# Two transformer-like blocks on one core: rate rows, wide decay products and a regrouped s5 input

## What is computed

```python
# gated delta rule, chunks of 64 tokens in the reference (the kernel takes 128)
g = jnp.cumsum(chunks(g), axis=-1)                 # g = -exp(a_log) * softplus(alpha_raw + dt_bias)
diff = g[..., :, None] - g[..., None, :]
decay = jnp.where(incl, jnp.exp(jnp.where(incl, diff, 0.0)), 0.0)
L = jnp.where(strict, jnp.einsum('bhnid,bhnjd->bhnij', kb, k) * decay, 0.0)
attn = jnp.einsum('bhnid,bhnjd->bhnij', q, k) * decay
...
# SSD, chunks of 128 tokens
adt = (dt * a)                                     # dt = softplus(dt_raw + dt_bias), per head
a_cs = jnp.cumsum(adt, axis=-1)
seg = a_cs[..., :, None] - a_cs[..., None, :]
lmat = jnp.exp(jnp.where(mask, seg, -jnp.inf))
y_diag = jnp.einsum('bcgls,bcghls,bcsghp->bclghp', cb, lmat, xdt)
...
# s5: a complex linear recurrence per group of 16 channels
bu = jnp.einsum('gpc,blgc->blgp', b_bar, ug)
h = linear_scan(jnp.broadcast_to(lam_bar, bu.shape), bu)
y = jnp.real(jnp.einsum('gcp,blgp->blgc', cmat, h)).reshape(bsz, seq, S5_WIDTH)
```

## Time and profile before

| | |
|---|---|
| median of 3 runs | 3497.77 us (3496.14 to 3498.61) |
| profiled execution | 3498.63 us, span 3496.8 us |
| granted clock, mean | 0.974 |
| busy | TensorE 96%, VectorE 42%, POOL 21%, ScalarE 20% |
| chain that ended last | TensorE 88%, VectorE 8%, ScalarE 2%, POOL 1% |
| first mixers, 0 to 800 us | TensorE busy 708.43, VectorE 461.88 us |
| second block's mixers, 1842 to 2256 us | TensorE busy 407.12, VectorE 224.15, POOL 0.81 us |

### The profile page before, as it was taken

How to read it: one execution, slowest core, us unless ns; L and a number is a source line. 1 busy time by engine, 2 the same in 40 slices (tenths; PEclk the granted TensorE clock), 3 DMA queues, 4 the chain that set the end, 5 groups by cost and what they waited for, 6 DMA issues and landing times.

```text
span 3496.8 us, 27790 instructions
## 1 busy us (share of the span) xinstructions
PE 3339.9 (96%) x10820; PEld 1650.8 (47%) x10820; DVE 1477.5 (42%) x2407; ACT 698.1 (20%) x1155; POOL 746.2 (21%) x623
## 2 busy tenths in 40 slices
PE   8989897899899999999999999999998999999996
PEld 3445463784344444444444555544553444444442
DVE  2375839552543443443326454422125333333313
ACT  3333332521110100101213234212223000000002
POOL 0000000003333423321210000021015524343203
PEclk9999898999999999999999999999998999999998
DMA  3211101052011111121212111222110111111112
GB/s 128 64 44 37 36 28 60 16 171 80 25 42 42 48 37 48 42 70 45 72 60 73 49 49 49 80 78 72 48 48 12 48 48 41 44 48 36 48 60 84
DMA packets 179635, 193.61 MB, mean 55 GB/s; under 512 B 5553, under 2 KB 172977, under 8 KB 178993
## 3 DMA queue, kind: packets, MB, share of 16 engines
q1 hardware_dynamic: 179504, 191.83, 17.1%
HBM read 185.53 MB, written 6.29 MB: 55 GB/s over the span
## 4 chain that ended last, share of the span: by engine, by line
PE 88%; DVE 8%; ACT 2%; POOL 1%; issue 1%; DMA 0%; SPq 0%; DVEq 0%; POOLq 0%
PE psum L1726 21%; PE psum L3261 19%; PE psum L178 12%; PE psum L2221 7%; PE psum L374 6%; PE psum L3288 3%; PE psum L1767 3%; PE psum L388 2%; PE psum L1755 2%; DVE arena L1392 1%; DVE arena L1292 1%; DVE arena L1290 1%; PE psum L526 1%; PE psum L3218 1%; PE psum L3179 1%
## 5 line engine op out<-in xcount | busy, mean ns | idle before, releaser
L1726 PE MATMUL psum<-arena 128*128 128x512 f32 x1736 | 748.3, 594 | 9.1 <-DVE arena L2014 9.0
L3261 PE MATMUL psum<-arena 128*128 128x512 f32 x1568 | 680.5, 597 | 13.4 <-ACT arena L3367 8.7
L1726 PEld LDWEIGHTS psum<-arena 128*128 128x128 f32 x1736 | 330.6, 191 | 426.5 <-issue 423.3
L275 POOL TENSOR_TENSOR arena<-arena 128x512 f32<-128x512 f32 (+1 forms) x310 | 372.8, 1236 | 590.3 <-DMA arena<-mlp_w 251.2
L3261 PEld LDWEIGHTS psum<-arena 128*128 128x128 f32 x1568 | 299.9, 192 | 394.1 <-issue 384.9
L178 PE MATMUL psum<-arena 128*128 128x512 f32 x1024 | 442.6, 592 | 0.0
L1937 DVE TENSOR_TENSOR arena<-arena,psum 128x512 f32<-128x512 f32 x336 | 221.2, 684 | 459.9 <-PE psum L1726 276.7
L3524 DVE TENSOR_TENSOR arena<-arena,psum 128x512 f32<-128x512 f32 x288 | 189.5, 684 | 515.0 <-PE psum L3261 316.1
L374 PE MATMUL psum<-arena 128*128 128x512 f32 x768 | 337.1, 599 | 3.6 <-DVE arena L1146 3.6
L178 PEld LDWEIGHTS psum<-arena 128*128 128x128 f32 x1024 | 194.6, 190 | 241.7 <-issue 241.3
L2221 PE MATMUL psum<-arena 128*128 128x512 f32 x576 | 254.8, 602 | 0.0
(11 more groups left out here) (449 smaller groups left out, 3166.3 us busy)
## 6 DMA issues: line engine op xcount, KB each, us to landing
arena<-w_in SPq DMA_DIRECT2D x42, 1024.0 KB, 5.3
arena<-mlp_w SPq DMA_DIRECT2D x36, 1024.0 KB, 5.2
arena<-w_out SPq DMA_DIRECT2D x16, 1024.0 KB, 5.0
arena<-w_ffn_gate SPq DMA_DIRECT2D x11, 1024.0 KB, 5.3
arena<-w_ffn_up SPq DMA_DIRECT2D x11, 1024.0 KB, 5.3
arena<-w_ffn_down SPq DMA_DIRECT2D x12, 768.0 KB, 4.4
arena<-w_ple_gate SPq DMA_DIRECT2D x8, 1024.0 KB, 5.1
arena<-xa_wq SPq DMA_DIRECT2D x8, 1024.0 KB, 5.0
```

Source lines behind the costliest of these rows:

```text
L275: return g.tensor_tensor(to[:, 0:kn, :], block_of(*a), block_of(*b), op)
L1726: mm = nc.tensor.matmul(ps, left, right, start=(k == 0), stop=(k == kn - 1))
L3261: mm = nc.tensor.matmul(ps, left, right, start=(k == 0), stop=(k == 3))
```

## The change

It makes five edits in the two mixer stages.

1. The rate weights come padded from 8 to 32 columns. The eight products go to four groups of 32 output partitions, two each, and the turning sums the four groups (`sel8` has a one wherever partition mod 32 equals the column). In the second block this takes the place of `steps_of`, split into `steps_of` and `step_tokens`, one unit apart, with a copy by ScalarE between.
2. POOL writes a x incl (`wide_rates`; in the second block a loop of its own) into SBUF, and one matmul with the mask `after` (s > t) gives g_t - g_s for four heads at once. The mask product and the bias are gone.
3. What lies above the diagonal is no longer masked by -1e30 (its exponent is 0). In the first block POOL multiplies the exps by `incl` (`masked_decays`), and VectorE waits for that; in the second VectorE multiplies CB by `incl` in PSUM.
4. ScalarE stores the s5 input u group by group, so that each group of tokens is contiguous.
5. Several counters share one semaphore.

```diff
 def rows_ab(h):
     ps = tiles.open(pe, "ab", h)
     for k in range(KD):
-        mm = nc.tensor.matmul(ps[0:8], w8[:, k, :], hn(k, h), start=(k == 0), stop=(k == KD - 1))
+        rows = slice(32 * (k % 4), 32 * (k % 4) + 32)
+        mm = nc.tensor.matmul(ps[rows], w8[:, k, :], hn(k, h), start=(k < 4), stop=(k >= 4))
...
 def dn_grams(h):
             ps = tiles.open(pe, "E", h, g + par)
-            nc.tensor.matmul(ps, const["ident"], rep(const["negmask"], HEADS), start=True, stop=False)
-            for c, e, n in of_part(g + par):
-                mm = nc.tensor.matmul(head(ps, n), col16(small["a16"], c, e).broadcast_to([P, P]), const["incl"],
-                                      start=False, stop=(n == 3))
-            tiles.close(mm)
+            pe.wait_ge(s["decay_step"], 8 * h + g + par + 1)
+            tiles.close(nc.tensor.matmul(ps, const["after"], rk[:, g + par, :], start=True, stop=True))
...
+def wide_rates(h):
+    pool.wait_ge(s["dn_dve"], 11 * h + 4)
+    a4 = small["a16"].rearrange("p (c i e) -> p c i e", i=2, e=2)
+    for m in range(4):
+        if h:
+            tiles.wait(pool, "O", "rw", 0, m)
+        a = a4[:, 2 * (m // 2):2 * (m // 2) + 2, :, m % 2].unsqueeze(3).broadcast_to([P, 2, 2, P])
+        g.tensor_tensor(quad(rk[:, m, :]), a, both(const["incl"]), ALU.mult).then_inc(s["decay_step"], 1)
+
+def masked_decays(h):
+    for m in range(4):
+        tiles.wait_taken(pool, "E", h, m)
+        x = quad(exps[m % 2])
+        g.tensor_tensor(x, x, both(const["incl"]), ALU.mult).then_inc(s["decay_step"], 1)
...
 # second block, TensorE
 def steps_of(h):
+    ps = tiles.open(pe, "dt_rows", h)
+    for k in range(KD):
+        rows = slice(32 * (k % 4), 32 * (k % 4) + 32)
+        mm = nc.tensor.matmul(ps[rows], w8[:, k, :], x_half(k, h), start=(k < 4), stop=(k >= 4))
+    tiles.close(mm)
+def step_tokens(h):
+    tiles.wait_taken(pe, "dt_rows", h)
     ps = tiles.open(pe, "dt", h)
     for c in range(CHUNKS):
-        for k in range(KD):
-            mm = nc.tensor.matmul(ps[:, c * SSD_HEADS:(c + 1) * SSD_HEADS], of_tile(x_half(k, h), c), w8[:, k, :],
-                                  start=(k == 0), stop=(k == KD - 1))
+        mm = nc.tensor.matmul(ps[:, c * SSD_HEADS:(c + 1) * SSD_HEADS], of_tile(dt_rows, c), cols_of("sel8", 8),
+                              start=True, stop=True)
...
 def before(h, c):                      # at its end, behind EG, CB and XT
+    for n in range(2):
+        pe.wait_ge(s["pool_made"], 2 * (4 * h + c) + n + 3)
+        ps = tiles.open(pe, "E", h, c, n)
+        tiles.close(nc.tensor.matmul(ps, const["after"], exps[c % 2][:, n * HALF:(n + 1) * HALF], start=True, stop=True))
...
 # second block, ScalarE
-        for e in range(4):
-            ee_ = 4 * half + e
-            ins = A(head(exps[c % 2], ee_), head(tiles.ps("E", h, c, half), e), ACT.Exp,
-                    bias=neg_g[:, c * SSD_HEADS + ee_:c * SSD_HEADS + ee_ + 1])
+        tiles.take(A(exps[c % 2][:, half * HALF:(half + 1) * HALF], tiles.ps("E", h, c, half), ACT.Exp), "E", h, c, half)
...
 # second block, VectorE
+    step.step(dve, v_.tensor_tensor(cb, cb, const["incl"].unsqueeze(1).broadcast_to([P, 2, P]), ALU.mult))
...
 # second block, POOL
+            for n in range(2 * CHUNKS):
+                h, c = n // CHUNKS, n % CHUNKS
+                if c == 0:
+                    pool.wait_ge(s["sd"], 6 * h + 3)
+                    if h:
+                        pool.wait_ge(s["ssd_out"], 4)
+                if n >= 2:
+                    tiles.wait(pool, "Y", (n - 2) // CHUNKS, (n - 2) % CHUNKS)
+                for half in range(2):
+                    a = a32[:, c * SSD_HEADS + 4 * half:c * SSD_HEADS + 4 * half + 4].unsqueeze(2).broadcast_to([P, 4, P])
+                    x = exps[c % 2][:, half * HALF:(half + 1) * HALF].rearrange("p (e t) -> p e t", e=4)
+                    g.tensor_tensor(x, a, const["incl"].unsqueeze(1).broadcast_to([P, 4, P]), ALU.mult).then_inc(s["pool_made"], 1)
...
 # s5
-                                x = u[i][rows, h * HALF + g:(h + 1) * HALF:GROUP]
+                                x = of_tile(u[i][rows, h * HALF:(h + 1) * HALF], g)
...
-                        nc.tensor.matmul(o, km[:, i, j, :], u[i][:, h * HALF + g - j:(h + 1) * HALF:GROUP], start=(j == 0), stop=False)
+                        nc.tensor.matmul(o, km[:, i, j, :], of_tile(u[i][:, h * HALF:(h + 1) * HALF], g - j), start=(j == 0), stop=False)
```

More of the change, by code:

```diff
@@ L801, in ab_rows @@
                 tiles.wait(act, "ab", h)
-                tiles.take(A(abrow, tiles.ps("ab", h)[0:8], ACT.Copy), "ab", h)
+                tiles.take(A(abrow, tiles.ps("ab", h), ACT.Copy), "ab", h)
             def q_squares(h):
@@ L892, in decays @@
                     for c, e, n in of_part(g):
[L893 removed]
+                        ins = A(head(exps[g % 2], n), head(tiles.ps("E", h, g), n), ACT.Exp, bias=col16(small["lnc"], c, e))
                     tiles.take(ins, "E", h, g)
@@ L2250, in before @@
                 cols = lambda e: a32[:, c * SSD_HEADS + e:c * SSD_HEADS + e + 1]
-                for n in range(2):
-                    ps = tiles.open(pe, "E", h, c, n)
-                    nc.tensor.matmul(ps, const["ident"], rep(const["negmask"], 4), start=True, stop=False)
-                    for e in range(4):
-                        mm = nc.tensor.matmul(head(ps, e), cols(4 * n + e).broadcast_to([P, P]), const["incl"],
-                                              start=False, stop=(e == 3))
-                    tiles.close(mm)
                 ps = tiles.open(pe, "EG", h, c)
@@ L2457, in first_tap, with step_rows @@
                       ).then_inc(s["tap0"], 1)
+            def step_rows(h):
+                tiles.wait(act, "dt_rows", h)
+                tiles.take(A(dt_rows, tiles.ps("dt_rows", h), ACT.Copy), "dt_rows", h)
             def silu(name, h):
@@ L2462, in silu, with take_as @@
                     A(dst[name][i], dst[name][i], ACT.Silu).then_inc(s["silu_ready"], 1)
-            def take_as(func, name, h, to, **kw):
+            def take_as(func, name, h, to, view=lambda ap: ap, **kw):
                 for i in range(2):
                     tiles.wait(act, name, h, i)
-                    tiles.take(A(to(i), tiles.ps(name, h, i), func, **{k: f(i) for k, f in kw.items()}), name, h, i)
+                    tiles.take(A(to(i), view(tiles.ps(name, h, i)), func, **{k: f(i) for k, f in kw.items()}), name, h, i)
             def scalars(h):
@@ L2486, in before @@
                 n = 4 * h + c
-                if c == 0:
-                    act.wait_ge(s["sd"], 6 * h + 5)
-                    if h:
-                        act.wait_ge(s["ssd_out"], 4)
-                if n >= 2:
-                    tiles.wait(act, "Y", (n - 2) // 4, (n - 2) % 4)
-                for half in range(2):
-                    tiles.wait(act, "E", h, c, half)
-                    for e in range(4):
-                        ee_ = 4 * half + e
-                        ins = A(head(exps[c % 2], ee_), head(tiles.ps("E", h, c, half), e), ACT.Exp,
-                                bias=neg_g[:, c * SSD_HEADS + ee_:c * SSD_HEADS + ee_ + 1])
-                    tiles.take(ins, "E", h, c, half)
                 if n >= 2:
@@ L2503, in before @@
                 tiles.take(A(eg[c % 2], tiles.ps("EG", h, c), ACT.Exp), "EG", h, c)
+                for half in range(2):
+                    tiles.wait(act, "E", h, c, half)
+                    tiles.take(A(exps[c % 2][:, half * HALF:(half + 1) * HALF], tiles.ps("E", h, c, half), ACT.Exp), "E", h, c, half)
             def inverse_root(to, key, sem, scale, bias):
@@ L2830, in s5_skip @@
                 tiles.wait(dve, "Y5", h, i)
-                x = u[i][:, h * HALF:(h + 1) * HALF]
-                tiles.take(v_.scalar_tensor_tensor(out_half(4 + i, h), x, col("s5_d_2", i), tiles.ps("Y5", h, i), ALU.mult, ALU.add), "Y5", h, i)
+                x, o = in_groups(u[i][:, h * HALF:(h + 1) * HALF]), in_steps(out_half(4 + i, h))
+                tiles.take(v_.scalar_tensor_tensor(o, x, col("s5_d_2", i), in_steps(tiles.ps("Y5", h, i)), ALU.mult, ALU.add), "Y5", h, i)
             def s5_gate(h):
@@ L3776, in constants @@
         "minus_incl": -1.0 * (s <= t),
-        "negmask": np.where(s <= t, 0.0, -1e30),
+        "after": s > t,
         "offmask": s // BLOCK < t // BLOCK,
@@ L3818, in column_layout @@
     offsets = np.where(one_head < HEADS, 0.0, bias[one_head % HEADS])
-    for name, row in (("dn_sgn", signs), ("dn_off", offsets), ("dn_alog16", np.tile(np.asarray(inputs["dn_a_log"]).reshape(-1), NC // 2)),
+    for name, row in (("dn_sgn", signs[0:8]), ("dn_off", offsets), ("dn_alog16", np.tile(np.asarray(inputs["dn_a_log"]).reshape(-1), NC // 2)),
                       ("ssd_off32", np.tile(np.asarray(inputs["ssd_dt_bias_2"]).reshape(-1), NC // 2)),
```

114 lines of the change are left out of this document (62 added, 52 removed).

## The result

| | before | after |
|---|---|---|
| median of the comparison | 3498.19 us (4 runs) | 3453.9 us (4 runs, 3452.71 to 3454.57) |
| profiled execution, its span | 3498.63, 3496.8 us | 3452.71, 3450.8 us |
| first mixers end | 774.32 us | 768.97 us |
| second block's mixers, start and end | 1842.64, 2256.07 | 1837.39, 2210.88 |

The ratio is 0.9873 [0.9856, 0.9891]: 44.3 us faster, where 50.7 were forecast. The time is 6.9 us above the forecast and inside the range. The stage rows (starts of the chain's pieces) say where: 5.35 us in the first mixers (7.1 forecast; 1.7 of the 5.35 are there before the first edited instruction, which starts at 101.25 instead of 102.92 us), nothing between, 39.9 in the second block's mixers (43.6 forecast), and 0.8 behind them. The range of the ratio is worth 38 to 50 us.

The account below looks back on a forecast made before the run. TensorE was taken to bound the kernel, without a break in the second block's mixers, with VectorE bounding parts of the first. Savings of 9.7, 13.2, 2.5, 13.1, 14.8 and -2.6 summed to 50.7 us, giving 3447; range 3438 to 3462.

Parts of the forecast that it names:

- A: First block's rate rows: four partition groups side by side save 4.9 us per half, 9.7 in all; bounds 0 and 10.4.
- B: Second block's rate columns: fewer, wider products save 13.2 us, and the clock no longer falling to 0.50 adds 2.5.
- C: Second block's decay products: 16 tiles each drop 0.89 us, 14.2, less 1.1 not passed on: 13.1; bounds 7 and 14.2.
- D: Second block's s5 products: a contiguous moving operand saves 8.0 us at L2357 and 6.8 at L2344, 14.8; bounds 0 and 16.
- E: First block's decay products: 0.6 us saved in the first half, 3.2 lost in the second: -2.6; bounds +4 and -16.
- The sign for the stage up to 606 us: First mixers: the prediction would be wrong if this stage did not come earlier by some 7 us.
- Rival 3: Rate products of both blocks: groups with 512 moving columns do not overlap, giving 3466 us; chance 0.05.
- TensorE still without a gap between 1842 and the tail: Second block's mixers: a sign expected if the prediction held, TensorE not waiting there before the tail.
- rival 1: s5 products: the strided output is what is slow, so they give only 6.8 us, 3455; chance 0.08.
- round trip: First block's second half: QK product, exps, POOL's mask, then VectorE again; last products end at 515.1 against 513.85 us.
- collision: First block's second half: POOL's first two masks fall on four VectorE operations reading SBUF twice, losing another 2.0 us.
- Rival 2: First mixers: all 16 new POOL operations slow VectorE through the shared port, 15.9 us lost instead of 2.0, 3461; chance 0.10.

Follow-up runs that it names:

- experiment 2: Changed kernel with all eight rate products sent to the same 32 output partitions, in both blocks: 3470.9 us.
- experiment 4: Changed kernel with the second block's rate columns computed as before, 32 matmuls a half with 8 moving columns: 3473.98 us.
- scan_later: Changed kernel with VectorE's first chunk of the second half put ahead of the s5 scan in the second block's mixers: 3453.12 us.
- v_first: Changed kernel with VectorE's first chunk ahead of the s5 scan and ScalarE's s5 input copies ahead of its square roots: 3449.97 us.
- experiment 3: Changed kernel with u stored in order of time again, so the s5 products move every fourth token: 3464.16 us.
- experiment 7: Changed kernel with contiguous s5 outputs alone, 3453.53 us; also with old first-block decay products, rate sums behind the next unit and scan behind the first chunk, 3447.15.
- experiment 1: Changed kernel with the first block's decay products as before (mask product, four products, no product on POOL): 3452.01 us.
- experiment 8: Changed kernel with later rate sums and no first-block exp mask, 3441.78 us; changed kernel with POOL's second-block products made four times, 3457.19; a third moved ScalarE's copies, 3449.97.
- experiment 9: Changed kernel with later rate sums, scan behind first chunk, s5 copies ahead of square roots, and POOL's first-block masks out of VectorE's way: 3436.81 us.
- experiment 6: Changed kernel with the rate sums of the first block's second half put behind the next unit: 3447.22 us.

## Why the prediction was right, and where it was off

| term | forecast | the trace of after |
|---|---|---|
| A, rate rows | 9.7 | 5.1 a half, 10.2 |
| B, dt columns and clock | 13.2 + 2.5 | 14.1 + 2.9 |
| C, decay products, second block | 14.2 - 1.1 | 14.2 - 4.3 (three new waits) |
| D, s5 products | 8.0 + 6.8 | 5.4 + 7.5 |
| E, decay products, first block | -2.6 | +0.8 - 3.5 = -2.7 |
| clock elsewhere | 0 | -3.5 and + 0.8 |
| start, ahead of every edit | 0 | + 1.7 |

The lines sum to some 46 us; the two spans differ by 46.0, the medians by 44.3. The last two lines are no merit of the prediction: without the 1.7 of the start the profiled time would be 3454.4, just outside the forecast's own narrow band (3441 to 3454), though well inside the range. The sign for the stage up to 606 us (some 7 us earlier) came out at 6.0 (L628 at 606.26, L626 at 600.24), with that 1.7 in it.

**What bounds the kernel** was read rightly: matmuls removed in the second block's mixers came out nearly one for one, and in the first mixers VectorE decided.

**A and B.** 0.1156 us a record against 0.131 forecast, and 0.435 before. Rival 3 fell with experiment 2. The clock's part was right in cause (experiment 4) and near in size (2.9, or 3.7 in experiment 4's execution, for 2.5).

**C** is the step that failed most. "TensorE still without a gap between 1842 and the tail" is wrong: I had gone through POOL's due times for the new product and through VectorE's tail, and allowed 1.1. But TensorE reaches XT of the second half's first chunk 3.5 us sooner by the decay tiles, which now stand behind it, and 3.7 sooner by the s5 inputs. Before, it had come there 4.2 us after ScalarE's first copy of the s5 inputs, which frees the PSUM tile; now it comes first and waits 2.9. ScalarE's order there is exps, two square roots, and only then the copies. VectorE's part was 0.7. scan_later, which moves VectorE's work alone, gave 0.5 of the stage back; v_first, which moves ScalarE's copies as well, 3.4. The loss is booked under C, but D has an equal share in it: with the slower inputs of experiment 3 the same waits are down to 0.3 with C's edit in place. In the tail, where I had taken off 1.1, nothing was lost: from the end of the last unit to the last products ahead of the 6.9 us wait it took 26.1 us before and 21.0 after. What I should have asked of each step of TensorE that moved earlier is who frees the tile eight places back.

**D.** The cause was right, rival 1 wrong by experiment 7 (297 ns against 296). The size of L2357's part was not: "48 x 0.12" took the pace of long runs of records. Short pieces of 2, 4 and 6 behind products of another shape cost 0.2 us each on top, strided or not, ten times (two of the twelve stand behind a unit), 2.0 us of the 2.6 that are missing. L2344's part came out at 0.0295 a record (forecast 0.033).

**E.** Both halves came out within 0.3 us inside the profiled executions (the medians of experiments 1 and 7 do not resolve them), and the two parts of the second one (round trip 1.2, collision 2.0) were found again at 1.3 and 2.1. Rival 2 is out as a size, and its mechanism is right: the Trainium skill (SBUF — State Buffer, two separate sides) calls the pair of ports an exclusive lock held for a whole instruction, and the trace agrees, 1.41 us becoming 2.42 and 0.22 becoming 1.20, while operations fed from PSUM stay at 2.47 for four. What I had missed is that the cost also stood in the kernel before: POOL's masks beside the inverses cost 3.9 us each, which the same rows had shown me. And the wide product is worth 0.2 us there, not the 0.9 a tile that it takes off TensorE, since the exps bound the pair (experiments 8 and 9).

**The clock.** 2.5 us were lost at 412 us, in a place that no edit touches: a wait grew from 1.9 to 3.5 us because TensorE came earlier. I had looked for clock given back and not for clock lost. That this is the cause is shown from two sides: experiment 6 takes the wait away by a unit, and experiment 2 takes away TensorE's gain and leaves the order as it is; both keep the clock and the 2.5 us. The other 1.0 of the table's 3.5 is 0.5 each at 349 us (L469, 3.66 against 3.14) and at 600 us (L626, 6.13 against 5.63), which no experiment touched; the 0.8 is the last products of the second mixers (5.87 against 6.63).

What stays open: why experiment 1's QK product waited at 493.9 us long enough for the clock to fall where the kernel before did not, and how often. One of its four runs was 6 us shorter (3445.65) than the other three, but only one execution has a trace.

## What to carry to other kernels

Take the removed matmuls at their own time, but then go through each place where TensorE now arrives sooner and ask for two things: which engine frees the PSUM tile it opens there, and whether a wait that it had grows, since a stretch at half clock may follow it. A POOL operation that reads two SBUF operands belongs where VectorE is fed from PSUM or idle; moving masks that were there before the change shortened each of two inverses by 3.9 us, of which the medians show about 1 us in all.

## What the runs showed of the hardware that I had not expected

- 32-column groups of fp32 matmuls overlap with 512 moving columns: 3.8 times in pace (6.98 us for 16 records in one group, 1.85 in four), with each record as long (594 and 598 ns).
- A moving operand with a stride of four fp32 costs 0.23 against 0.11 us a record of 128 columns; an output with that stride costs nothing (296 and 297 ns).
- The granted clock was 0.50 behind products with 8 moving columns although TensorE was busy throughout, and behind a wait of 3.5 us; it stayed at 1.00 behind waits of 1.9 and 1.7 us at the same place.
- The same work ahead of the first rate rows ended between 99.76 and 103.26 us from one kernel's profile to the next, so differences of 3 us between two profiled executions can come from there alone.
